# The first mixer of a two-block network on one core: mean squares taken from x by tokens, loads in the order of the channel groups, one band product per token block, and its norm closed by halves of the tokens

## What is computed

```python
def pool_mixer(h, w_pool, scale):          # four groups of 256 channels, windows 2, 4, 8, 16
    mean = (csum[:, 1:, sl] - csum[:, lo, sl]) / cnt
    diffs.append(mean - hf[..., sl])
    y = jnp.einsum('bsgc,gcd->bsgd', d, w_pool)
    return y * scale
h = rms_norm(x, mix_pre_g[0])              # x * rsqrt(mean(x*x over channels) + eps) * g
x = x + rms_norm(pool_mixer(h, pool_w[0], pool_scale[0]), mix_post_g[0])
f = conv_glu_ffn(rms_norm(x, ffn_pre_g[0]), ...)
```

## Time and profile before

| | us |
|---|---|
| median of three runs | 1689.5 |
| the profiled execution | 1685.19 |
| its span | 1683.5 |
| PE busy | 1610.1 (96% of the span) |
| DVE busy | 1031.8 (61%) |
| ACT busy | 701.2 (42%) |
| POOL busy | 202.9 (12%) |
| start of PE's first product | 13.6 |

### The profile page before, as it was taken

The page is one execution under the profiler, slowest core; times in us unless marked ns, Lnnn a source line. Parts: engine busy times, 40 slices in busy tenths (PEclk is TensorE's granted clock), DMA queues, the critical chain, the costliest instruction groups (busy, mean ns, idle before and its releaser), DMA issues.

```text
span 1683.5 us, 21246 instructions
## 1 busy us (share of the span) xinstructions
PE 1610.1 (96%) x7986; PEld 1298.2 (77%) x7986; DVE 1031.8 (61%) x1931; ACT 701.2 (42%) x1370; POOL 202.9 (12%) x169
## 2 busy tenths in 40 slices
PE   6899999999998899999999999999998999999996
PEld 6688888888876687888888887766666788888875
DVE  4766666653768677666763376676666455553364
ACT  3444444333436645444442343344334343343252
POOL 2421111100002211111110000000011001110011
PEclk9899999999999999999999999999999999999998
DMA  4033333334121122333332424221110223333321
GB/s 147 26 106 95 94 101 95 106 100 138 39 65 32 38 88 82 94 100 95 99 97 92 141 97 125 56 50 40 39 45 26 88 90 99 96 98 97 98 88 62
DMA packets 89342, 141.55 MB, mean 84 GB/s; under 512 B 8468, under 2 KB 28436, under 8 KB 89112
## 3 DMA queue, kind: packets, MB, share of 16 engines
q1 hardware_dynamic: 86464, 133.56, 26.7%
q10 hardware_dynamic: 2776, 6.63, 1.2%
HBM read 138.06 MB, written 2.10 MB: 83 GB/s over the span
## 4 chain that ended last, share of the span: by engine, by line
PE 89%; DVE 6%; issue 2%; ACT 1%; POOL 1%; DMA 0%; SPq 0%; DVEq 0%; POOLq 0%; ACTq 0%
PE ps L423 23%; PE ps L425 23%; PE ps L424 23%; PE ps L1864 2%; PE ps L1865 2%; PE ps L1866 2%; PE ps L1546 1%; PE ps L1569 1%; PE ps L1589 1%; PE ps L436 1%; PE ps L443 1%; PE ps L438 1%; PE ps L437 1%; DVE Hl L538 1%; DVE X L738 1%
## 5 line engine op out<-in xcount | busy, mean ns | idle before, releaser
L408 DVE TENSOR_TENSOR wl<-raw,wh 128x512 fp32r<-128x512 f32 (+2 forms) x443 | 328.5, 745 | 429.5 <-ACT wh L399 429.3
L399 ACT ACTIVATE wh<-raw 128x512 fp32r<-128x512 f32 (+2 forms) x443 | 276.3, 627 | 593.2 <-PE ps L425 582.2
L423 PE MATMUL ps<-Hh,wh 128*128 128x512 f32 x1256 | 499.4, 398 | 13.5 <-DVE Hl L538 8.2
L424 PE MATMUL ps<-Hl,wh 128*128 128x512 f32 x1256 | 492.2, 392 | 0.0
L425 PE MATMUL ps<-Hh,wl 128*128 128x512 f32 x1256 | 492.1, 392 | 0.0
L423 PEld LDWEIGHTS ps<-Hh,wh 128*128 128x128 f32 x1256 | 237.5, 189 | 69.1 <-DVE Hl L538 10.6
L424 PEld LDWEIGHTS ps<-Hl,wh 128*128 128x128 f32 x1256 | 237.8, 189 | 50.7 <-issue 1.9
L425 PEld LDWEIGHTS ps<-Hh,wl 128*128 128x128 f32 x1256 | 237.5, 189 | 50.7
L423 PE MATMUL ps<-AH,wh 128*128 128x512 f32 x416 | 161.8, 389 | 0.0
L424 PE MATMUL ps<-AL,wh 128*128 128x512 f32 x416 | 161.8, 389 | 0.0
L425 PE MATMUL ps<-AH,wl 128*128 128x512 f32 x416 | 161.8, 389 | 0.0
(11 more groups left out here) (297 smaller groups left out, 1970.8 us busy)
## 6 DMA issues: line engine op xcount, KB each, us to landing
raw<-in_w_in SPq DMA_DIRECT2D x216, 256.0 KB, 2.7
raw<-in_w_out SPq DMA_DIRECT2D x104, 256.0 KB, 2.6
raw<-in_w_up SPq DMA_DIRECT2D x64, 256.0 KB, 2.6
raw<-in_w_down SPq DMA_DIRECT2D x32, 256.0 KB, 2.6
raw<-in_w_q SPq DMA_DIRECT2D x16, 256.0 KB, 2.6
raw<-in_w_o SPq DMA_DIRECT2D x16, 256.0 KB, 2.6
raw<-in_w_pg SPq DMA_DIRECT2D x16, 256.0 KB, 2.6
X<-in_xT SPq DMA_DIRECT2D x8, 256.0 KB, 6.5
```

Of the source, the lines that this page charges most:

```text
L399: e.activation(split_in[n][0][:, 0:width], raws[n % NRAW][:, 0:width], ACT.Copy, scale=1.0 if gain is None else gain).then_inc(s_hi, 1)
L408: e.tensor_tensor(wl[:, 0:width], raw, wh[:, 0:width].bitcast(F32), ALU.subtract).then_inc(s_lo, 1)
L423: e.matmul(b, wh[:, o:o + w], xh, start=k == 0, stop=False, skip_group_check=joined)
L424: e.matmul(b, wh[:, o:o + w], xl, start=False, stop=False, skip_group_check=joined)
```

## The change

**Loads.** x tiles 2g and 2g+1 are followed by pool weight g. Behind them x is loaded a second time, untransposed, tokens on partitions, as four transfers of 512 KB into M, which is free then. Band matrix and identity move from ACT's queue to SP's, behind these. Only the first 40 columns of `cols` are loaded at first, on ACT's queue; the rest comes last on SP's, before piece 4. ACT runs a Square of one element ahead of its first wait for data.

**Mean squares.** ACT squares each token block of 1024 channels and sums along it in the same instruction. DVE's variance scales by 1/1024. The squares and additions of DVE and GpSimd and PE's one-column products for them are gone.

**Band.** The band matrix holds 144 columns for a block: its own 128 and 16 of the next. One product per token block replaces the two; the last block has 128.

**Closing.** Channel tiles 0 to 3 run over all tokens, tiles 4 to 7 by halves, in four PSUM banks. ACT copies tiles 0 and 2 into M, DVE 1 and 3, with the product of pool scale and post gain, made once on GpSimd. From there variance, root, diagonal and spread run by halves, `dve_new_rhs` and `pe_first_group` take for this border the same form as for the others, and GpSimd's additions go over to DVE. Pieces 4 to 9 are split ahead of the first group: ACT makes four high parts between the halves and two behind them, DVE three low parts between the halves and three behind.

The diff, cut to its core and moved left:

```diff
...
-band = sub("band", [P, 4, 272], 0)
+band = sub("band", [P, 4, 288], 0)
 Z = sub("Z", [P, 4, D], 4608)
+xsq = [sub(f"xsq{n}", [P, 2, S], 24576 + 4096 * n) for n in range(4)]
+pgain = st[:, 136:144]
...
 more = [[(sub(f"xh{b}{i}", [P, NPIECE], o + 4096 * i, F32R), sub(f"xl{b}{i}", [P, NPIECE], o + 4096 * i + 2048,
-          F32R)) for i in range(7)] for b, o in enumerate((0, 57856, 0))]
+          F32R)) for i in range(7)] for b, o in enumerate((57856, 0, 57856, 0))]
 KCR, VCR, KS, VS, KW, VW, Q2, MQ, MK, MV, MO = 0, 1, 2, 3, 4, 5, 6, 10, 14, 18, 22
...
-            upto = max(upto, min(n + 3 + min(n - grow + 1, 7), new + 7))
+            upto = max(upto, min(n + 3 + min(n - grow + 1, 7), new + (5 if n < 4 else 7)))
...
+    halved = 3 if j < 4 else 0
     for half in range(2):
         for k in range(halved):
...
-POST_T = ((0, 1, 2, 3, 4, 5, 6, 7),) + ((5, 6, 7, 0, 0, 1, 2, 6),) * 3
+POST_T = ((5, 6, 7, 0, 1, 2, 3, 4),) + ((5, 6, 7, 0, 0, 1, 2, 6),) * 3
+def post_gain(q, c):
+    return pgain[:, c:c + 1] if q == 0 else col(POST_GAIN[q], c)
...
+def added_at(q, half, i):
+    return 2 * half + i if q == 0 else 6 * q - 2 + 3 * half + i
 def add_square(e, q, i, half):
-    n = 6 * (q - 1) + 3 * half + i
+    n = added_at(q, half, i)
     c = slice(256 * half, 256 * half + 256)
-    e.wait_ge(s_merge, MERGES[q])
+    if q == 0:
+        e.wait_ge(s_pair, 1)
+    else:
+        e.wait_ge(s_merge, MERGES[q])
     e.wait_ge(s_psq, tile_at(q, 4 + i, half))
     if n > 0:
         e.wait_ge(s_qsum, n)
...
     if c == 0:
         e.wait_ge(s_spread, CHAIN_AT[POST_CHAIN[q]] - (2 if half == 0 else 1))
...
+        if q == 0:
+            e.wait_ge(s_pea, 2)
+    t = slice(0, S) if half is None else slice(256 * half, 256 * half + 256)
+    e.tensor_tensor(M[:, c, t], M[:, c, t], spread_roots(q)[:, t], ALU.mult).then_inc(s_psc, 1)
...
 def dve_new_rhs(e, q, j, k):
-    if k == 0 and q > 0:
+    if k == 0:
...
-    elif q > 0:
+    else:
         if k < 5:
             scale_m(e, q, k + 3)
             rhs_low(e, j, k + 2)
...
+    for g in range(4):
+        for c in (2 * g, 2 * g + 1):
+            e.dma_start(X[:, c, :], A["xT"][c * P:(c + 1) * P, :]).then_inc(s_x[c], 16)
+        load(e, g)
+    for n in range(4):
+        e.dma_start(M[:, 2 * n:2 * n + 2, :].rearrange("p a c -> p (a c)"),
+                    A["x"][n * P:(n + 1) * P, :]).then_inc(s_xt[n], 16)
+    e.dma_start(band[:, :, :].rearrange("p g n -> p (g n)"), const("band")).then_inc(s_band, 16)
+    e.dma_start(ident[:, :], A["const"][:, 0:P]).then_inc(s_ident, 16)
+    e.dma_start(cols[:, NCOLS0:NCOLS], A["cols"][:, NCOLS0:NCOLS]).then_inc(s_cols, 16)
+    for n in range(4, NP):
         load(e, n)
 def pool_init(e):
+    e.memset(mean[:, :], 1.0 / D).then_inc(s_init, 1)
     e.memset(ones[:, :], 1.0)
-    e.memset(mean[:, :], 1.0 / D)
     e.memset(st[:, 128:132], -0.5)
     for t in ts[:-1]:
         e.memset(t[:, 0:2], 0.0)
     e.memset(ts[-1][:, 0:2], 0.0).then_inc(s_init, 1)
 def act_init(e):
...
+    e.dma_start(cols[:, 0:NCOLS0], A["cols"][:, 0:NCOLS0]).then_inc(s_cols0, 16)
     e.wait_ge(s_init, 1)
...
+    e.activation(st[:, 144:145], mean[:, 0:1], ACT.Square)
+    e.wait_ge(s_cols0, 16)
+    e.wait_ge(s_init, 2)
+Z_BANK = (4, 5, 6, 7, 0, 1, 2, 3)
 def act_pool_mixer(e):
     for c in range(KD):
         e.wait_ge(s_x[c], 16)
         e.activation(Hh[:, c, :], X[:, c, :], ACT.Copy, scale=col("mix_pre0", c)).then_inc(s_hh, 1)
-        if c in (1, 3):
+        if c % 2:
             split_high(e, c // 2)
...
+    for n in range(4):
+        e.wait_ge(s_xt[n], 16)
+        i = e.activation(xsq[n][:, :, :], M[:, 2 * n:2 * n + 2, :], ACT.Square, accum_out=st[:, 8 + n:9 + n])
+    i.then_inc(s_stat, 1)
     for pair in range(2):
         for n in (0, 2):
             e.wait_ge(s_z, 4 * pair + n + 1)
             e.wait_ge(s_rs, 1)
             e.activation(Z[:, n, pair * 512:pair * 512 + 512], banks[Z_BANK[4 * pair + n]][:, :], ACT.Copy,
                          scale=st[:, 4 + n:5 + n]).then_inc(s_za, 1)
...
+    e.wait_ge(s_pg, 1)
+    for c in (0, 2):
+        for i in range(2):
+            post_square(e, 0, c + i, banks[4 + c + i], (s_bnd, c + i + 1), col("pool_scale", c + i))
+        e.activation(M[:, c, :], banks[4 + c][:, :], ACT.Copy, scale=pgain[:, c:c + 1]).then_inc(s_pea, 1)
+    for half in range(2):
+        c = slice(256 * half, 256 * half + 256)
+        for i in range(4):
+            e.wait_ge(s_bnd, 4 + 4 * half + i + 1)
+            e.activation(T[POST_T[0][4 + i]][:, c], banks[i][:, c], ACT.Square,
+                         scale=col("pool_scale", 4 + i)).then_inc(s_psq, 1)
+        if half == 0:
+            for n in range(4, 8):
+                split_high(e, n)
+    split_high(e, 8)
+    split_high(e, 9)
+    e.wait_ge(s_cols, 16)
 def dve_pool_mixer(e):
-    e.wait_ge(s_cols, 16)
+    e.wait_ge(s_cols0, 16)
     for c in range(KD):
         e.wait_ge(s_hh, c + 1)
         e.scalar_tensor_tensor(Hl[:, c, :], X[:, c, :], col("mix_pre0", c), Hh[:, c, :].bitcast(F32),
                                ALU.mult, ALU.subtract).then_inc(s_hl, 1)
-        if c in (1, 3):
+        if c % 2:
             split_low(e, c // 2)
...
+    e.wait_ge(s_init, 2)
+    e.wait_ge(s_stat, 1)
+    e.tensor_scalar(st[:, 0:4], st[:, 8:12], 1.0 / D, EPS, ALU.mult, ALU.add).then_inc(s_var, 1)
     for pair in range(2):
         for n in (1, 3):
             e.wait_ge(s_z, 4 * pair + n + 1)
             e.wait_ge(s_rs, 1)
             e.tensor_scalar(Z[:, n, pair * 512:pair * 512 + 512], banks[Z_BANK[4 * pair + n]][:, :],
                             st[:, 4 + n:5 + n], None, ALU.mult).then_inc(s_zd, 1)
...
+    e.wait_ge(s_pg, 1)
+    post_take(e, 0, 1, banks[5])
+    post_pair(e, 0, 0)
+    post_take(e, 0, 3, banks[7])
+    post_pair(e, 0, 2)
     e.wait_ge(s_ident, 16)
+    for half in range(2):
+        for i in range(4 - half):
+            if i < 2:
+                add_square(e, 0, i, half)
+            half_take(e, 0, i, half)
+            if half and i == 1:
+                half_diagonal(e, 0, 0)
+        if half == 0:
+            for n in range(4, 7):
+                split_low(e, n)
+            half_variance(e, 0, 0)
+    for n in range(7, 10):
+        split_low(e, n)
+    e.wait_ge(s_cols, 16)
 def gpsimd_pool_mixer(e):
...
+    e.wait_ge(s_cols0, 16)
+    e.tensor_tensor(pgain, cols[:, COLS["pool_scale"][0]:COLS["pool_scale"][0] + 8],
+                    cols[:, COLS["mix_post0"][0]:COLS["mix_post0"][0] + 8], ALU.mult).then_inc(s_pg, 1)
     root(e, 0)
+def band_product(e, c, blocks):
+    g, o = c // 2, c * P
+    b = banks[(4 + c) % 8]
+    for n in blocks:
+        w = 144 if n < 3 else P
+        f = 0 if n == 0 else 144
+        m = e.matmul(b[:, n * P:n * P + w], Z[:, n, o:o + P], band[:, g, f:f + w], start=n == 0, stop=True,
+                     skip_group_check=True)
+    m.then_inc(s_bnd, 1)
+def mean_of_half(e, half):
+    e.wait_ge(s_qsum, added_at(0, half, 2))
+    half_square(e, 0, half, T[5], False, False)
+    e.wait_ge(s_psq, tile_at(0, 6, half))
+    half_square(e, 0, half, T[POST_T[0][6]], False, False)
+    e.wait_ge(s_psq, tile_at(0, 7, half))
+    half_square(e, 0, half, T[POST_T[0][7]], False, True)
 def pe_pool_mixer(e):
-    e.wait_ge(s_init, 1)
+    e.wait_ge(s_init, 2)
     for g in range(4):
-        wh, wl = spls[g]
+        wh, wl = split_in[g]
         e.wait_ge(s_hl, 2 * g + 2)
         e.wait_ge(s_lo, g + 1)
         for n in range(4):
-            if g == 2 and n == 3:
-                e.wait_ge(s_var, 1)
             out = banks[Z_BANK[4 * (g // 2) + n]][:, 256 * (g % 2):256 * (g % 2) + 256]
             for k in range(2):
                 xh, xl = (h[:, 2 * g + k, n * P:(n + 1) * P] for h in (Hh, Hl))
...
                 m.then_inc(s_z, 1)
             elif n == 3:
                 m.then_inc(s_used, 1)
...
     e.wait_ge(s_band, 16)
...
+    for c in range(4):
+        if c == 0:
+            e.wait_ge(s_za, 2)
+            e.wait_ge(s_zd, 2)
+        band_product(e, c, range(4))
+    e.wait_ge(s_za, 4)
+    e.wait_ge(s_zd, 4)
+    for half in range(2):
+        for i in range(4):
+            if half:
+                e.wait_ge(s_pev, taken_at(0, 4 + i, 0))
+            band_product(e, 4 + i, (2 * half, 2 * half + 1))
+            if half and i == 1:
+                mean_of_half(e, 0)
+        if half == 0:
+            e.wait_ge(s_pair, 2)
+            half_square(e, 0, 0, T[7], True, False)
+            half_square(e, 0, 1, T[7], True, False)
     e.wait_ge(s_ident, 16)
-    spread(e, 1, banks[POST_BANK])
+    half_spread(e, 0, 0)
+    mean_of_half(e, 1)
...
 def gpsimd_ffn(e, l):
     j, q, G = FFN_J[l], FFN_Q[l], NG[l]
     if l < 2:
-        for half in range(2 if q else 0):
+        for half in range(2):
             half_root(e, q, half)
...
 c[:, b:b + P] = np.where(inside, 1.0 / np.minimum(q + 1, w), 0.0) - (q == p)
-c[:, b + P:b + 2 * P] = np.where(inside, 1.0 / w, 0.0) - (q == p)
```

(5 more changed lines are left out.)

200 lines of the change are left out of this document (42 added, 158 removed).

## The result

The changed kernel takes 1667.5 us (median of four runs, 1664.6 to 1671.1) against 1689.0 for the kernel before on the same chip (1686.4 to 1690.9): ratio 0.9875, 95% interval 0.9851 to 0.9898. The forecast was 1667.5, range 1659 to 1677.

A forecast was written before the change was run, and what follows sets the result against it. PE's dense products bound all past the first FFN group, so only the second group's start counts: 88.7 to 66.8, saving 21.9 us. 1685.2 becomes 1663.3 profiled, 1667.5 against the median; range 1659 to 1677.

The forecast's parts named there:

- Start: Loads before the first pool product: weight 0 lands near 5.4 us, first product at 6.9 instead of 13.6.
- Pool products: The 96 pool weight products on PE: 13.6 us without waiting for data, ending at 20.5 instead of 36.1.
- Mean squares: Second x load, squares and root ahead of the band products: Z scaled at 21.7, PE idle 1.2 us.
- Band products: Band stage on PE: 1.17 us a tile instead of 1.57, bounds 1.08 and 1.57; stage from 21.7 to 33.1.
- Closing: Norm before the first FFN: DVE's queue decides, and the first FFN product comes at 39.0 instead of 62.8.
- signs of being wrong: Listed signs include late Z, PE waiting between band halves, DVE's weight parts ahead of a needed operand, second group after 72.
- First group: First group of the first FFN: 27.8 us instead of 25.9, ending at 66.8, with low clock at its start.
- Nothing moved behind it: The stretch from the second FFN group on stays at 1594.8 us; longer would mean weights, not products, bound it.
- The rule weighed: Skill's rule: clock falls only behind longer idle gaps, saving 24 us; forecast followed the trace row, counting low clock at 39.
- the root was 0.3 us late and not 3: Rival, 12%: slow x transfers or squares put Z at 25; 3.3 us wait plus 2 for clock, 1672.8 us.
- no transfer came slowly: Rival, 2%: x by tokens arrives at a small fraction of the rate; at 60 GB/s the kernel takes 1696.8 us.
- DVE's queue: Rival, 15%: weight parts between halves delay the closing; first FFN product at 43, group 28.5, total 1672.2 us.

The follow-up runs named there:

- experiment 6: Also written x_table: changed kernel without the one-element dummy Square that brings ScalarE's table load ahead of the data; 1664.6 us, one run.
- experiment 1: Changed kernel with all eight x tiles loaded ahead of the four pool weights; 1668.6 us, ratio 0.9882; run again, 1672.2 us.
- experiment 9: Changed kernel with DVE's weight parts moved out of the closing, one block's squares on DVE, and filler products in threes; 1664.8 us, ratio 0.9858.
- Experiment 2: Changed kernel with the old mean squares (ACT, DVE, GpSimd additions, PE sums) and no second load of x; 1676.1 us, ratio 0.9922.
- experiment 7: Changed kernel with half 0's variance ahead of one DVE weight part and three later parts behind DVE's first new operands; 1667.9 us, ratio 0.9871.
- x_order_2: Second run of the changed kernel with all x tiles loaded ahead of the pool weights; 1672.2 us, ratio 0.9891.
- experiment 4: Kernel before with the new loads, squares, band products and early table load, but without the closing by halves; 1674.1 us, ratio 0.9914.
- a_again: The changed kernel run once more, unchanged; 1668.1 us, ratio 0.9876.
- x_warm: Changed kernel with eleven unread filler products where PE waits in the closing and first group; 1665.0 us, ratio 0.9863.
- x_band: Changed kernel with two band products per token block again (128 and 16 columns); 1670.1 us, median of five, ratio 0.9881.
- experiments 5: Experiment 5, the run x_warm: changed kernel with eleven unread filler products where PE waits; 1665.0 us, ratio 0.9863.

## Why the prediction was right, and where it was not

The median is the predicted one to 0.1 us, but not every step is. On the profiled execution the forecast was 1663.3 and 1666.8 was measured: 2.1 of the 3.5 were lost ahead of the second group, all of them in the first group, and 1.4 behind it. The median agrees because I added the 4.3 us between before's profile and its median of three, and after's profile lay only 0.7 below its own. That was luck, of the size of the spread from run to run.

**Start: right in kind, 0.5 late.** Weight 0 landed at 5.9, not 5.4. I put the table load's cover at up to 1.28; experiment 6 shows 0.75 at the first product, and the wait for Z takes it up. The same wait takes up part of what the order of the loads gives (experiment 1).

**Pool products: right.** 96 in 12.9 us, without a pause; forecast 13.6. The slow spacing lasted 2.7 us, not 4.7. The other two profiles of the changed kernel took 13.2 and 14.2, and end at 20.7 and 21.3; so the wait for Z, 1.73 us here, is longer or shorter by chance. The stretch moved 392 GB/s, against 377 in the earlier trace rows.

**Mean squares: right, and in the way forecast.** "Three of four are done while the last lands" held: the third square and its sum were done at 17.8, and the last block landed at 17.91 (17.6 in the two other profiles; forecast 17.5). Square and sum took 1.06 + 0.18 for my 1.15 + 0.19. The mean was there at 19.2 for 18.9, the root at 20.45 for 20.2, and Z at 22.1 for 21.7. What paces this stage is the second load of x, and squaring faster does not shorten it (experiment 9). Experiment 2 shows 8.5 us for this part; my share for it and the pool products was 7.7.

**Band products: the size was too cautious.** I took 1.17 us a tile; 1.00 was measured, below my lower bound of 1.08. A 144 wide product costs no more than a 128 wide one did in the earlier trace rows; 48 in 6.03 us is 0.126 each. The full tiles and half 0 thus took 6.0 us for my 7.0. Sums and half 1 behind them took 4.7 for my 4.4, and the stage began 0.4 late, so its end was only 0.3 early.

**Closing: right time, half the reason.** "Here DVE decides" names one of two limits. DVE's rows come a little ahead of the forecast (diagonal 33.8 for 34.6, weight parts to 36.3 for 36.8). One of my signs of being wrong did show: the three weight parts stand ahead of the scaling of M, 36.30, though PE's spread was done at 35.5. But with them out of the way (experiment 7) PE's one-column records at the low clock hold the end as long. I had these at 1.2 us for twelve; they took 2.56, because the clock was down already at 34, where I had counted it low only at 39. With the records at the full clock and DVE as it was, the stretch from first band to first FFN product is 16.3 and 16.2 us (x_table, x_order_2); with DVE's order changed alone 16.9; with both 15.2 (experiment 9); in the changed kernel 16.7. Two limits of about equal length stood side by side. Band and closing together gave 10.0 us ahead of the group for my 9.4; the halves have 7.0 of that by experiment 4.

**First group: the step that failed.** I gave it 27.8 us, with one fall of the clock at its start. It took 30.1, with a second, 3.5 us long, behind the 1.02 us in which PE waits for DVE's additions. I had seen that lateness and counted it at its own length, 1.3, not for what a pause can set off. Without the second fall the same program takes 28.3 (a_again), 0.5 over my figure; without either, 26.9 (x_warm). The price of the lateness is thus 1 us in some executions and near 3 in others, and near 3 in eight of the ten profiles with that pause.

**"Nothing moved behind it": right, with a caveat.** Nothing shows that the 1.4 us longer rest are weights that come late: it holds the same 7600 products, and over all 14 profiles its length goes with the low clock inside it (without the last 20 us):

| profile | low clock in the rest | length |
|---|---|---|
| before | 23.8 | 1594.8 |
| x_table | 23.9 | 1595.1 |
| after | 30.7 | 1596.2 |
| a_again | 33.6 | 1598.7 |
| x_order_2 | 43.9 | 1602.7 |
| x_band | 44.1 | 1602.7 |

These are six of the 14, with the lowest and the highest. The slope over all is about 0.4 us a microsecond of low clock. The spread is 8 us between programs that run the same products there. It is a correlation over profiles; no run changed the clock of the rest on purpose.

**The rule weighed.** The row was the better guide: the clock was down around the closing and at the start of the first group in all three profiles of the changed kernel, though PE never paused longer than 1.73 us once it had begun. The saving of 24 that the prediction worked out by the rule of the Trainium skill (TensorE: Matmul & The Clock Gate, "HAM oscillation — how this bites in real kernels") was not reached; experiments 5 and 9 come nearest, with the second group at 65.7 and 65.1 (23.0 and 23.6 us ahead of before's). But the earlier trace rows is no rule either. At the layer's next closing the same code paused 0.92 us before and after the change. Before, the clock fell for 3.5 us; after, the window from 408 to 414, which holds that pause, reads 1.00:

```profile
410.74 0.39 PE L437 MATMUL ps<-Hh,wh 128*128 128x256 f32 x1 [0.92 <-DVE Hl L540]
...
408.00:414.00 6.00, 4.95 (x38) 4.70 (x37) 5.25 (x17) 1.64 (x4) 0.70 (x1) 1.00 0.00 1
```

A short pause may bring a fall; it need not.

**The parts.** Undone one at a time they cost, in time, 3.5 (loads), 8.5 (mean squares), 3.0 (band) and 7.0 (closing): 22.0 us, against 22.1 for the whole; by the second group 3.8, 7.3, 3.7 and 4.5: 19.3 of 20.6. They nearly add up, as they should if each lies on the path in its own stage. The agreement is closer than the numbers can bear: each is a difference of means of four to twelve runs that spread over 3 to 8 us. The rivals did not happen: the root was 0.3 us late and not 3, no transfer came slowly, and DVE's queue put the first FFN product at 38.9 and not 43.
